# q, k and v of the second block as three 1024-column groups with three steps of seven products each

## The chip, the cores and the metric

The kernel runs on one core of a Trainium2 chip. The metric is the device time of one execution in microseconds, as a median of several runs. The engines are TensorE (PE in the profile, its weight loads PEld), VectorE (DVE), ScalarE (ACT), GpSimd (POOL) and SyncE (SP), which issues the loads.

## What is computed

Two transformer blocks follow one another on 256 tokens of 2048 features in float32. The parts that matter here, shortened:

```python
def rms_norm(x, g):
    y = x * lax.rsqrt(jnp.mean(x * x, axis=-1, keepdims=True) + EPS)
    return y * g

def first_block(x, ...):                         # DEPTH = 1, mixer 0
    h = rmsnorm(x, norm_g[i, 0])
    h = fox_attention(h, fox_w_in[j], fox_b_f[j], fox_w_out[j])
    x = x + rmsnorm(h, norm_g[i, 1])
    h = sqrelu_mlp(rmsnorm(x, norm_g[i, 2]), mlp_w1[i], mlp_w2[i])
    return x + rmsnorm(h, norm_g[i, 3])

def hybrid_layer(x, norm_g, w_in, ...):          # the second block
    h = rms_norm(x, norm_g)
    proj = h @ w_in
    q, k, v, z_a, u_b, v_b, z_b, g_a, g_b = jnp.split(proj, cuts, axis=-1)
    q = rms_norm(q.reshape(B, S, 8, 128), q_norm_g)
    k = rms_norm(k.reshape(B, S, 8, 128), k_norm_g)
    att = moba_attention(q, k, v.reshape(B, S, 8, 128))
    y_a = (att * silu(z_a)) @ w_proj_a
    sgu = spatial_gating(gelu(u_b), gelu(v_b), sgu_norm_g, w_s, b_s)
    y_b = (sgu * silu(z_b)) @ w_proj_b
    merged = sigmoid(g_a) * y_a + sigmoid(g_b) * y_b
    return x + merged @ w_out
```

The change concerns `h @ w_in` for the first 3072 columns of `w_in` (q, k and v), the head norms' sums of squares of q and k, and the end of the v_b columns, which come just before them.

## The kernel before

**Products in parts.** Every float32 matrix product is made in three matmuls on values split in a rounded part and a rest: x_hi w_hi + x_lo w_hi + x_hi w_lo. The activations lie turned (features on partitions) in `h_both` or `a_both`. The weights come as a stream of 622 chunks of 128x1024 floats (512 KB) through a ring of four slots `raw`. For each chunk SyncE issues the load as soon as VectorE has made `w_lo` of the chunk four before in the same slot; ScalarE makes `w_hi` (`split`, L935), but not before TensorE has finished the chunk four before (`chunk_done`); VectorE makes `w_lo = raw - w_hi` (`rest`, L1412). The call `next_split(c)` or `next_rest(c)` handles chunk c + 4. Each engine runs its program in the written order, and semaphores tie them together.

**Groups.** In the phase `qkv` (64 chunks) TensorE first does v_b in `first_groups` (chunks 0 to 15, 1024 columns in two halves, `group_bank[0]` and `group_bank[1]`), where the first chunks run beside the turning of the normed input. Chunks 8 to 11 finish the first half and 12 to 15 the second. Then `rows_of_rstd(3)` (L659) makes rows of the row scales `rstd` in bank 6. It waits for `diagonal(3)`, which VectorE makes when GpSimd has computed `rstd` (`pow_norm`) from the sums of squares that `scale_of_rows(2)` adds up. Then come q, k and v as six groups of 512 columns, each 8 chunks, two groups to a turn of a loop (`group_pair`, chunks 16 to 63). After each group ScalarE squares the two banks (L1307), and VectorE scales them into `qkv` (L1967) and adds the squares up by head (L1970). The stage behind is `sgu_uz` (feature tiles).

**v_b's gelu.** Each half is scaled and squared by ScalarE, multiplied out by VectorE, put through tanh by ScalarE and summed by head, with roundings of later chunks between.

**Wide groups.** The MLP's second product is already done in groups of 1024 columns, 16 chunks, each with three steps of seven products (`seven_products`). A step takes a 2x2 arrangement of blocks (two feature blocks by two halves of the tokens, two feature blocks by two halves of the columns) and makes seven block products in place of eight, by Winograd's form of Strassen's rule. It needs four sums of activations for each step (`x_forms`, rounded by ScalarE into `x_form_hi`, VectorE's rest in `x_form_lo`), three sums of weights for each step and group (`outer_sums`, `inner_sum`, `last_sum`; `form_hi` on ScalarE, `form_rest` on VectorE), and a join of the four extra sums at the group's end (`join_seven`, then `plain_drain`). The three sums and the difference written back over `raw` come before the split of the step's first chunk.

## Time and profile before

| | us |
|---|---|
| median of 3 runs | 1782.65 (1782.48 to 1783.97) |
| the profiled execution, whole | 1782.02 |
| its span, first to last instruction | 1780.3 |
| TensorE busy | 1772.9 |
| VectorE busy | 1234.5 |
| ScalarE busy | 869.1 |
| GpSimd busy | 139.6 |

Times in the profile are us from the span's start. A matmul's end is modelled and overlaps the next one's start, so that distances between starts tell the pace. In the timeline rows neighbouring operations of one kind are merged, with their count at the end. In the trace of this execution chunk 8 of the phase `qkv` begins at 1117 us and chunk 16, the first of q, at 1139 us.

### The profile page before, as it was taken

To read this page: it belongs to the slowest core of one execution; us is meant where nothing else is said; L and a number is where in the kernel's file an instruction comes from. 1 tells how busy PE (TensorE), PEld (TensorE's weight loads), DVE (VectorE), ACT (ScalarE), POOL (GpSimd) and SP (SyncE) were. 2 spreads that over 40 slices of the span, in tenths; PEclk is the share of its full clock that TensorE was granted. 3 is DMA by queue.
4 is the path that set the end of the run, shared out by engine and by line. 5 is a ranking of instruction groups with operands and counts; after the bars stand their busy time and mean duration, and the time that the engine had idled before them with its cause. 6 is when DMAs were issued, how large, how long until landed. Compare 5 with 4: busy or idle time off the path is not lost.

```text
span 1780.3 us, 26370 instructions
## 1 busy us (share of the span) xinstructions
PE 1772.9 (100%) x8818; PEld 1503.3 (84%) x8818; DVE 1234.5 (69%) x1623; ACT 869.1 (49%) x1169; POOL 139.6 (8%) x190
## 2 busy tenths in 40 slices
PE   9999999999999999999999999999999999999999
PEld 8888888888888888888888887888888888888887
DVE  6567777556888788778887868755688655555654
ACT  7434444446555445445554555744444445553442
POOL 1012121000001000000000000100013011000000
PEclk9999999999999999999999999999999999999999
DMA  8665455556568656855775586555555655555554
GB/s 326 206 219 163 165 165 165 190 169 193 171 212 228 200 186 214 232 191 189 214 235 189 189 251 199 191 196 190 179 186 177 201 174 180 172 175 189 186 189 154
DMA packets 99111, 347.24 MB, mean 195 GB/s; under 512 B 11472, under 2 KB 11872, under 8 KB 98656
## 3 DMA queue, kind: packets, MB, share of 16 engines
q1 hardware_dynamic: 93392, 333.23, 56.8%
q0 software_dynamic: 4784, 12.60, 3.3%
q8 instruction: 47, 0.77, 0.2%
q10 hardware_dynamic: 864, 0.44, 0.1%
q14 instruction: 24, 0.20, 0.0%
HBM read 336.77 MB, written 2.11 MB: 190 GB/s over the span
## 4 chain that ended last, share of the span: by engine, by line
PE 95%; DVE 2%; DMA 1%; issue 1%; ACT 1%; POOL 0%; SPq 0%; DVEq 0%; ACTq 0%; POOLq 0%
PE bank L457 39%; PE bank L436 23%; PE bank L441 12%; PE bank L750 5%; PE bank L751 5%; PE bank L749 5%; DMA raw<-in_stream 1%; PE bank L473 1%; PE bank L507 1%; PE bank L586 1%; DVE w_lo L1412 1%; PE bank L627 1%; PE bank L642 1%; ACT w_hi L935 1%; PE bank L633 0%
## 5 line engine op out<-in xcount | busy, mean ns | idle before, releaser
L1412 DVE TENSOR_TENSOR w_lo<-raw,w_hi 128x1024 fp32r<-128x1024 f32 x620 | 755.3, 1225 | 423.5 <-ACT w_hi L935 420.1
L935 ACT ACTIVATE w_hi<-raw 128x1024 fp32r<-128x1024 f32 x620 | 649.3, 1056 | 622.5 <-PE bank L457 336.6
L457 PE MATMUL bank<-w_hi,h_both 128*128 128x512 f32 x1544 | 480.0, 392 | 0.0
L436 PE MATMUL bank<-h_both,w_hi 128*128 128x512 f32 x1792 | 432.8, 394 | 0.4 <-DVE gate L1815 0.4
L436 PEld LDWEIGHTS bank<-h_both,w_hi 128*128 128x128 f32 x1792 | 330.6, 188 | 65.9 <-issue 0.9
L457 PEld LDWEIGHTS bank<-w_hi,h_both 128*128 128x128 f32 x1544 | 288.0, 188 | 58.3
L457 PE MATMUL bank<-w_lo,h_both 128*128 128x512 f32 x772 | 301.1, 390 | 0.0
L441 PEld LDWEIGHTS bank<-h_both,w_lo 128*128 128x128 f32 x1792 | 229.8, 191 | 8.7
L441 PE MATMUL bank<-h_both,w_lo 128*128 128x256 f32 x1792 | 232.5, 283 | 0.0
L457 PE MATMUL bank<-w_hi,a_both 128*128 128x512 f32 x576 | 178.5, 391 | 0.0
L457 PEld LDWEIGHTS bank<-w_lo,h_both 128*128 128x128 f32 x772 | 145.0, 188 | 30.4
L457 PEld LDWEIGHTS bank<-w_hi,a_both 128*128 128x128 f32 x576 | 107.5, 188 | 21.8
L749 PE MATMUL bank<-w_hi,a_both 128*128 128x512 f32 x322 | 125.6, 390 | 0.2 <-DVE w_lo L1412 0.2
L750 PE MATMUL bank<-w_hi,a_both 128*128 128x512 f32 x322 | 125.4, 390 | 0.0
L751 PE MATMUL bank<-w_lo,a_both 128*128 128x512 f32 x322 | 125.4, 389 | 0.0
L457 PE MATMUL bank<-w_lo,a_both 128*128 128x512 f32 x288 | 112.3, 390 | 0.0
L1173 ACT ACTIVATE a_both<-gate 128x256 fp32r<-128x256 f32 (+1 forms) x56 | 23.4, 418 | 139.6 <-DVE gate L1714 139.6
L749 PEld LDWEIGHTS bank<-w_hi,a_both 128*128 128x128 f32 x322 | 60.5, 188 | 13.5 <-issue 1.2
L751 PEld LDWEIGHTS bank<-w_lo,a_both 128*128 128x128 f32 x322 | 60.5, 188 | 12.5
L750 PEld LDWEIGHTS bank<-w_hi,a_both 128*128 128x128 f32 x322 | 60.5, 188 | 12.3
L457 PEld LDWEIGHTS bank<-w_lo,a_both 128*128 128x128 f32 x288 | 54.1, 188 | 11.3
L2238 POOL DMA_DIRECT2D wide<-scaled x21 | 18.4, 1000 | 540.6 <-ACT scaled L1212 540.6
(237 smaller groups left out, 1384.5 us busy)
## 6 DMA issues: line engine op xcount, KB each, us to landing
raw<-in_stream SPq DMA_DIRECT2D x622, 512.0 KB, 3.5
wide<-scaled POOLq DMA_DIRECT2D x21, 256.0 KB, 4.9
res<-in_x SPq DMA_DIRECT2D x4, 512.0 KB, 7.9
rowg<-in_norm_rows POOLq DMA_DIRECT2D x2, 1024.0 KB, 8.1
gate<-cum_rows POOLq DMA_DIRECT2D x1, 2048.0 KB, 8.3
out<-wide SPq DMA_DIRECT2D x8, 256.0 KB, 5.1
wide<-gate POOLq DMA_DIRECT2D x7, 256.0 KB, 8.6
gate<-in_x_turned SPq DMA_DIRECT2D x5, 256.0 KB, 6.4
```

The costliest lines, as they stand in the source:

```text
L436: pe.matmul(tile_sum[b][:, :], w_hi[:, slot + half, k * P:(k + 1) * P], h_both[:, 8 * half + k, :], start=half == 0 and k == 0, stop=False)
L441: mm = pe.matmul(tile_sum[b][:, 0:TOK], w_lo[:, slot + half, k * P:(k + 1) * P], h_both[:, 8 * half + k, 0:TOK], start=False, stop=half == ...
L457: mm = pe.matmul(dst[t][:, :], xt[:, k0 + 2 * j + k, tt], wt[:, slot, w], start=j == 0 and k == 0 and n == 0, stop=last and k == 1 and n == 2)
L473: mm = pe.matmul(dst[t][:, :], xt[:, 2 * j + k, tt], wt[:, slot, w], start=j == 0 and k == 0 and n == 0, stop=j == GROUP_CHUNKS - 1 and k ...
L507: mm = pe.matmul(group_bank[0][t][:, :], xt[:, 2 * j + k, t * P:(t + 1) * P], wt[:, j % RING, w], start=first, stop=False)
L749: pe.matmul(dst[:, :], x_parts[0], w_parts[0], start=start, stop=False)
L750: pe.matmul(dst[:, :], x_parts[1], w_parts[0], start=False, stop=False)
L751: return pe.matmul(dst[:, :], x_parts[0], w_parts[1], start=False, stop=stop)
L935: nc.scalar.activation(w_hi[:, slot, :], raw[:, slot, :], ACT.Copy).then_inc(hi_ready, 1)
L1173: nc.scalar.activation(one(a_hi, i * 2 + b), relu2[b], ACT.Copy).then_inc(ff_hi, 1)
L1412: nc.vector.tensor_tensor(w_lo[:, slot, :], raw[:, slot, :], w_hi[:, slot, :].bitcast(F32), ALU.subtract).then_inc(lo_ready, 1)
L2238: pool.dma_start(group_sum[:, t, start:start + GROUP_COLS], src, accum_op=ALU.add).then_inc(added[t][n], 16)
```

## The change

q, k and v become three wide groups of 1024 columns and 16 chunks, each with three steps of seven products, on banks `h_bank`. The shared functions take the activations, the form tiles and the banks as arguments now. The tiles for the forms lie in the space of `a_both`, which is free in this phase. The input forms are made from `h_hi + h_lo` by `h_forms`, between the roundings of chunks 12 to 15, and rounded by ScalarE between its splits. `rows_of_rstd(3)` moves two chunks forward, in front of chunk 14, and the copy of its rows (`keep_rows(2)`) into the first half of gelu, since bank 6 is one of the first group's banks. Roundings for the first wide group are woven into the second half of gelu. The results are joined in `h_part`, and ScalarE squares them head by head with accumulation (q and k only) and scales them into `qkv` (`scale_qkv`). VectorE's scaling and reductions of q, k and v go. The kernel's stream holds the same weights in another order. The core of the diff:

```diff
+        h_part = [gate_flat[:, 2048 + n * 512:2560 + n * 512] for n in range(4)]
+        h_sum = [gate_flat[:, 2048 + b * 256:2304 + b * 256] for b in range(2)]
+        qkv_forms = Forms(in_a("h_w_raw", 0, [3, GROUP_COLS], F32)[:, :, :], in_a("h_w_hi", 1536, [3, GROUP_COLS]),
+                          in_a("h_w_lo", 3072, [3, GROUP_COLS]), in_a("h_x_raw", 7680, [4, P], F32)[:, :, :],
+                          in_a("h_x_hi", 4608, [STEPS, 4, P]), in_a("h_x_lo", 6144, [STEPS, 4, P]), h_part)
...
+        h_bank = [[bank[2], bank[3], bank[7], bank[6]], [bank[0], bank[1], bank[5], bank[4]]]
...
+            def qkv_group(i):
+
+                c = FIRST["qkv"] + 16 + 16 * i
+                w = WIDE_GROUPS + i
+                plain, seven = h_bank[i % 2], h_bank[1 - i % 2]
+                if i:
+                    joined(w - 1)
+                else:
+                    pe.wait_ge(group_taken[0], 8)
+                for j in range(0, WIDE_CHUNKS, 2):
+                    pair = PAIR_ORDER[j // 2]
+                    if j in SEVEN_AT:
+                        if i:
+                            pe.wait_ge(join_step, 8 * w)
+                        else:
+                            pe.wait_ge(group_taken[1], 8)
+                        seven_products(c, j, SEVEN_AT.index(j), w, plain, seven, (h_hi, h_lo), qkv_forms,
+                                       STEPS * FF_GROUPS)
                         continue
                     for k in range(2):
-                        wide_chunk(c, j + k, 2 * pair + k, plain, g * 8 + 20 if n == 0 else 0)
+                        wide_chunk(c, j + k, 2 * pair + k, plain, (h_hi, h_lo),
+                                   {} if i else {3: lambda: pe.wait_ge(rows_ready, 2)})
...
-            first_groups(FIRST["qkv"], 6, 2)
-            rows_of_rstd(3)
-            with pe.Fori(1, 4) as i:
-                group_pair(FIRST["qkv"] + i * 16, i + 6, h_hi, h_lo)
+            first_groups(FIRST["qkv"], 6, 2, {(1, 6): lambda: rows_of_rstd(3)})
+            for i in range(QKV_WIDE):
+                qkv_group(i)
+            joined(WIDE_GROUPS + QKV_WIDE - 1)
 
...
             for m in range(4):
                 next_split(c + 8 + m)
+                if m < STEPS:
+                    act.wait_ge(x_form_step, 4 * STEPS * FF_GROUPS + 6 * m + 6)
+                    nc.scalar.activation(qkv_forms.x_hi[:, m, :, :], qkv_forms.x_raw, ACT.Copy).then_inc(x_form_hi_ready, 1)
...
+                vb_split(n, 2)
+                vb_split(n, 3)
+
+            def scale_qkv(i, t):
+
+                for n in range(2):
+                    block = 2 * t + n
+                    act.wait_ge(join_step, 8 * (WIDE_GROUPS + i) + block + 5)
+                    if i < 2:
+                        if 4 * i + block >= 2:
+                            act.wait_ge(qkv_sq, 4 * i + block - 1)
+                        for head in range(4):
+                            ins = nc.scalar.activation(gelu_a[:, n, head * P:(head + 1) * P],
+                                                       h_part[block][:, head * P:(head + 1) * P], ACT.Square,
+                                                       scale=rstd[:, t:t + 1],
+                                                       accum_out=head_sq[:, t, i * 8 + 4 * n + head:i * 8 + 4 * n + head + 1])
+                        ins.then_inc(qkv_sq, 1)
+                    start = i * 1024 + n * GROUP_COLS
+                    nc.scalar.activation(qkv[:, t, start:start + GROUP_COLS], h_part[block], ACT.Copy,
+                                         scale=rstd[:, t:t + 1]).then_inc(qkv_in, 1)
+
+            act.wait_ge(vb_sums, 4)
+            for i in range(QKV_WIDE):
+                for j in range(0 if i else RING, WIDE_CHUNKS):
+                    wide_split(c + 16 + 16 * i, WIDE_GROUPS + i, j, qkv_forms, h_bank[1 - i % 2])
+                    if i and j < 2:
+                        scale_qkv(i - 1, j)
+            for t in range(NT):
+                scale_qkv(QKV_WIDE - 1, t)
...
+            def wide_step(c, w, q, forms, drain=None):
+
+                at = SEVEN_AT[q]
+                step = STEPS * w + q
+                outer_sums(step, c + at, at % RING, forms)
+                if drain:
+                    drain(0, 0)
+                inner_sum(step, at % RING, forms)
+                if drain:
+                    drain(0, 1)
+                last_sum(step, at % RING, forms)
+                if drain:
+                    drain(1, 0)
+                    drain(1, 1)
+                for k in range(2):
+                    rest(c + at - RING + k, (at + k) % RING)
+                form_rest(step, forms)
+                for k in range(2, 4):
+                    rest(c + at - RING + k, (at + k) % RING)
+
+            def wide_join(c, w, seven, part):
+
+                rests(c + 12, range(2))
+                join_seven(w, seven, part)
+                rests(c + 12, range(2, RING))
...
+            def h_forms(q):
+
+                done = 4 * STEPS * FF_GROUPS + 6 * q
+                for b in range(2):
+                    kt = 2 * SEVEN_PAIRS[q] + b
+                    nc.vector.tensor_tensor(h_sum[b], h_hi[:, kt, :].bitcast(F32), h_lo[:, kt, :].bitcast(F32),
+                                            ALU.add).then_inc(x_form_step, 1)
+                a11, a21 = [h_sum[0][:, t * P:(t + 1) * P] for t in range(NT)]
+                a12, a22 = [h_sum[1][:, t * P:(t + 1) * P] for t in range(NT)]
+                s1, s2, s3, s4 = [qkv_forms.x_raw[:, f, :] for f in range(4)]
+                dve.wait_ge(x_form_step, done + 2)
+                nc.vector.tensor_tensor(s1, a21, a22, ALU.add).then_inc(x_form_step, 1)
+                nc.vector.tensor_tensor(s3, a11, a21, ALU.subtract).then_inc(x_form_step, 1)
+                dve.wait_ge(x_form_step, done + 3)
+                nc.vector.tensor_tensor(s2, s1, a11, ALU.subtract).then_inc(x_form_step, 1)
+                dve.wait_ge(x_form_step, done + 5)
+                nc.vector.tensor_tensor(s4, a12, s2, ALU.subtract).then_inc(x_form_step, 1)
+
+            def h_forms_lo(q):
+
+                dve.wait_ge(x_form_hi_ready, STEPS * FF_GROUPS + q + 1)
+                nc.vector.tensor_tensor(qkv_forms.x_lo[:, q, :, :], qkv_forms.x_raw,
+                                        qkv_forms.x_hi[:, q, :, :].bitcast(F32),
+                                        ALU.subtract).then_inc(x_form_ready, 1)
+
+            dve.wait_ge(chunk_done, c)
             next_rest(c + 8)
+            h_forms(0)
             next_rest(c + 9)
             scale_of_rows(2)
+            h_forms_lo(0)
+            h_forms(1)
             next_rest(c + 10)
+            h_forms_lo(1)
+            h_forms(2)
             next_rest(c + 11)
+            h_forms_lo(2)
             diagonal(3)
...
                     next_rest(c + 13)
+                    keep_rows(2)
+                else:
+                    next_rest(c + 17)
...
+                    outer_sums(STEPS * WIDE_GROUPS, c + 20, 0, qkv_forms)
+                    inner_sum(STEPS * WIDE_GROUPS, 0, qkv_forms)
+                    last_sum(STEPS * WIDE_GROUPS, 0, qkv_forms)
+                else:
+                    form_rest(STEPS * WIDE_GROUPS, qkv_forms)
+                    next_rest(c + 18)
+                    next_rest(c + 19)
+
+            for i in range(QKV_WIDE):
+                for q in range(0 if i else 1, STEPS):
+                    wide_step(c + 16 + 16 * i, WIDE_GROUPS + i, q, qkv_forms,
+                              (lambda t, n: qkv_drain(i - 1, t, n)) if i and q == 0 else None)
+                wide_join(c + 16 + 16 * i, WIDE_GROUPS + i, h_bank[1 - i % 2], h_part)
+            for t in range(NT):
+                for n in range(2):
+                    qkv_drain(QKV_WIDE - 1, t, n)
+
+
+            dve.wait_ge(qkv_in, 4 * QKV_WIDE)
...
-    parts += [paired_groups(v_b)] + [token_groups(m) for m in (q, k, v)]
+    parts += [paired_groups(v_b)] + [wide_groups(m) for m in (q, k, v)]
```

Line numbers in the changed kernel differ from those of before.

Where TensorE stands at the end of v_b, chunks 14 and 15 and the row scales (`qk_norm,ones`), before, from the last matmuls of chunk 15 to the first of q:

```order
L457 MATMUL bank<-w_lo,h_both 128x512
L457 MATMUL bank<-w_hi,h_both 128x512 x2
L457 MATMUL bank<-w_lo,h_both 128x512
L457 MATMUL bank<-w_hi,h_both 128x512 x2
L457 MATMUL bank<-w_lo,h_both 128x512
L659 MATMUL bank<-qk_norm,ones 128x128 [waits diag_ready]
L659 MATMUL bank<-qk_norm,ones 128x128
L841 UNCONDITIONAL_BRANCH
L841 ISA
L447 ISA [waits group_taken0]
L457 MATMUL bank<-w_hi,h_both 128x512 [waits lo_ready]
```

and in the changed kernel, from the end of chunk 13 to chunk 14:

```order
L472 MATMUL bank<-w_lo,h_both 128x512
L472 MATMUL bank<-w_hi,h_both 128x512 x2
L472 MATMUL bank<-w_lo,h_both 128x512
L472 MATMUL bank<-w_hi,h_both 128x512 x2
L472 MATMUL bank<-w_lo,h_both 128x512
L676 MATMUL bank<-qk_norm,ones 128x128 [waits diag_ready,h_ready]
L676 MATMUL bank<-qk_norm,ones 128x128
L472 MATMUL bank<-w_hi,h_both 128x512 [waits lo_ready]
L472 MATMUL bank<-w_hi,h_both 128x512
L472 MATMUL bank<-w_lo,h_both 128x512
L472 MATMUL bank<-w_hi,h_both 128x512 x2
```

The wait for `diag_ready` stood behind chunk 15 and stands behind chunk 13 now.

VectorE in the same place, before, from the roundings of chunks 11 to 13 to the diagonal (`qk_norm<-ident,rstd`):

```order
L1412 TENSOR_TENSOR w_lo<-raw,w_hi 128x1024 [waits hi_ready] x3
L1474 TENSOR_REDUCE sq_all<-sq_sum 128x2 [waits sumsq_ready]
L1412 TENSOR_TENSOR w_lo<-raw,w_hi 128x1024 [waits hi_ready] x2
L1479 TENSOR_SCALAR qk_norm<-ident,rstd 128x128 [waits rstd_ready]
L1479 TENSOR_SCALAR qk_norm<-ident,rstd 128x128
L1925 TENSOR_SCALAR mean_sq<-rstd 128x2
```

and now, the last lap: chunk 14's rounding, the low part of the second set, the third set (`h_x_raw`), chunk 15's rounding and the diagonal:

```order
L1486 TENSOR_TENSOR w_lo<-raw,w_hi 128x1024 [waits hi_ready]
L2029 TENSOR_TENSOR h_x_lo<-h_x_raw,h_x_hi 128x512 [waits x_form_hi_ready]
L2013 TENSOR_TENSOR gate<-h_both 128x256 x2
L2019 TENSOR_TENSOR h_x_raw<-gate 128x128 [waits x_form_step]
L2020 TENSOR_TENSOR h_x_raw<-gate 128x128
L2022 TENSOR_TENSOR h_x_raw<-h_x_raw,gate 128x128 [waits x_form_step]
L2024 TENSOR_TENSOR h_x_raw<-gate,h_x_raw 128x128 [waits x_form_step]
L1486 TENSOR_TENSOR w_lo<-raw,w_hi 128x1024 [waits hi_ready]
L2029 TENSOR_TENSOR h_x_lo<-h_x_raw,h_x_hi 128x512 [waits x_form_hi_ready]
L1553 TENSOR_SCALAR qk_norm<-ident,rstd 128x128 [waits rstd_ready]
L1553 TENSOR_SCALAR qk_norm<-ident,rstd 128x128
L2046 TENSOR_SCALAR mean_sq<-rstd 128x2
```

Between each rounding and the next there are now seven operations on the input forms, with a wait for ScalarE's rounding (`x_form_hi_ready`).

ScalarE at a group's end before: the fourth split of a ring and the two squares of a 512-column group, with the loop's register work:

```order
L935 ACTIVATE w_hi<-raw 128x1024 [waits raw_landed2,chunk_done]
L933 REGISTER_ALU
L935 ACTIVATE w_hi<-raw 128x1024 [waits raw_landed3,chunk_done]
L1306 REGISTER_ALU
L1307 ACTIVATE gate<-bank,rstd 128x512 [waits qkv_sums]
L1306 REGISTER_ALU
L1307 ACTIVATE gate<-bank,rstd 128x512 [waits qkv_sums]
```

and now at the start of k, from the split of its chunk 4 (which waits for `form_step`) on:

```order
L978 ACTIVATE w_hi<-raw 128x1024 [waits raw_landed0,chunk_done,form_step]
L1366 ACTIVATE gate,head_sq<-gate,rstd 128x128 [waits join_step]
L1366 ACTIVATE gate,head_sq<-gate,rstd 128x128 x3
L1372 ACTIVATE wide<-gate,rstd 128x512
L1366 ACTIVATE gate,head_sq<-gate,rstd 128x128 [waits join_step]
L1366 ACTIVATE gate,head_sq<-gate,rstd 128x128 x3
L1372 ACTIVATE wide<-gate,rstd 128x512
L978 ACTIVATE w_hi<-raw 128x1024 [waits raw_landed1,chunk_done]
L1233 ACTIVATE h_w_hi<-h_w_raw 128x1536 [waits forms_done,form_step]
L1366 ACTIVATE gate,head_sq<-gate,rstd 128x128 [waits qkv_sq,join_step]
L1366 ACTIVATE gate,head_sq<-gate,rstd 128x128 x3
L1372 ACTIVATE wide<-gate,rstd 128x512
```

The squares by head (`gate,head_sq`, four to a block) and the scaled copies (`wide<-gate,rstd`) stand between the splits of chunks 4 and 5, and again behind the rounding of the weight forms, in front of the split of chunk 6.

## Rows read from the trace of the kernel before

**Rows 1.** The page: busy time of the engines, and the clock slices (40).
```profile
PE 1772.9 (100%) x8818; PEld 1503.3 (84%) x8818; DVE 1234.5 (69%) x1623; ACT 869.1 (49%) x1169; POOL 139.6 (8%) x190
...
PEclk9999999999999999999999999999999999999999
```
**Rows 2.** Waits of TensorE: who waited for whom, us in total, times, longest.
```profile
PE bank L500 <- POOL ident L2152: 1.7, 1, 1.7
```
**Rows 3.** Timeline of TensorE: start us, duration us, engine, line, operation, out<-in, count.
```profile
1128.06 0.62 PE L457 MATMUL bank<-w_hi,h_both 128*128 128x512 f32 x2
...
1133.50 0.62 PE L457 MATMUL bank<-w_hi,h_both 128*128 128x512 f32 x2
...
1138.95 0.61 PE L659 MATMUL bank<-qk_norm,ones 128*128 128x128 f32 x4
1139.31 0.48 PE L457 MATMUL bank<-w_hi,h_both 128*128 128x512 f32 x1
```
**Rows 4.** Timeline of VectorE under v_b; in brackets its idle time before.
```profile
1121.54 1.23 DVE L1412 TENSOR_TENSOR w_lo<-raw,w_hi 128x1024 fp32r<-128x1024 f32 x1 [1.15 <-ACT w_hi L935]
...
1125.05 0.15 DVE L1474 TENSOR_REDUCE sq_all<-sq_sum 128x2 f32<-128x8 f32 x1
1126.63 1.80 DVE L1412 TENSOR_TENSOR w_lo<-raw,w_hi 128x1024 fp32r<-128x1024 f32 x1 [1.43 <-ACT w_hi L935]
...
1130.49 0.48 DVE L1479 TENSOR_SCALAR qk_norm<-ident,rstd 128x128 f32<-128x128 f32 x2
```
**Rows 5.** Timeline of VectorE, input forms of the MLP.
```profile
478.27 0.42 DVE L1717 TENSOR_TENSOR a_both<-gate,a_both 128x256 fp32r<-128x256 f32 x1 [0.48 <-ACT a_both L1173]
478.62 0.28 DVE L1736 TENSOR_TENSOR wide<-gate 128x128 f32<-128x128 f32 x1
...
479.55 1.22 DVE L1412 TENSOR_TENSOR w_lo<-raw,w_hi 128x1024 fp32r<-128x1024 f32 x1
480.68 0.69 DVE L1725 TENSOR_TENSOR x_form_lo<-wide,x_form_hi 128x512 fp32r<-128x512 f32 x1
```
**Rows 6.** Timeline of ScalarE, the same place.
```profile
479.67 0.63 ACT L1182 ACTIVATE x_form_hi<-wide 128x512 fp32r<-128x512 f32 x1 [0.48 <-DVE wide L1741]
```
**Rows 7.** Timeline of ScalarE, start of a wide group of the MLP.
```profile
533.88 1.05 ACT L935 ACTIVATE w_hi<-raw 128x1024 fp32r<-128x1024 f32 x1
534.83 1.47 ACT L1198 ACTIVATE form_hi<-gate 128x1536 fp32r<-128x1536 f32 x1
536.21 0.71 ACT L1212 ACTIVATE scaled<-scaled,rstd_sq 128x512 f32<-128x512 f32 x1
536.82 0.71 ACT L1212 ACTIVATE gate<-gate,rstd_sq 128x512 f32<-128x512 f32 x1
```
**Rows 8.** Timeline of GpSimd under v_b.
```profile
1126.26 1.09 POOL L2260 TENSOR_SCALAR_AFFINE_SELECT gate<-gate 128x1024 f32<-128x1024 f32 x1
```
**Rows 9.** Timeline of VectorE: first and last of gelu's second half, and the copy after.
```profile
1141.39 0.43 DVE L1931 TENSOR_SCALAR gate<-gate 128x512 f32<-128x512 f32 x1
...
1146.40 0.41 DVE L1484 COPY rstd_rows<-bank 128x256 f32<-128x256 f32 x1
```
**Rows 10.** Timeline of VectorE, start of a wide group of the MLP.
```profile
530.13 0.68 DVE L1762 TENSOR_TENSOR gate<-raw 128x512 f32<-128x512 f32 x1
...
534.93 2.35 DVE L1412 TENSOR_TENSOR w_lo<-raw,w_hi 128x1024 fp32r<-128x1024 f32 x2
537.21 1.75 DVE L1780 TENSOR_TENSOR form_lo<-gate,form_hi 128x1536 fp32r<-128x1536 f32 x1
```
**Rows 11.** Timeline of ScalarE, exponentials with accumulation.
```profile
1423.24 0.38 ACT L957 ACTIVATE prob<-logit,neg_max 128x128 f32<-128x128 f32 x1
1423.53 0.19 ACT L957 ACTIVATION_READ_ACCUMULATOR prob<-logit,neg_max 128x1 f32 x1
1423.62 0.49 ACT L959 ACTIVATE prob<-logit,neg_max 128x256 f32<-128x256 f32 x1
```
**Rows 12.** The page, DMA issues: KB each, median us to landing.
```profile
raw<-in_stream SPq DMA_DIRECT2D x622, 512.0 KB, 3.5
```

More of the change, by code:

```diff
@@ L13 @@
+import collections
 from contextlib import ExitStack
@@ L42 @@
 WIDE_GROUPS = 7
+QKV_WIDE = 3
 EPS = 1e-6
@@ L770, in wide_chunk @@
                     for n in range(2):
[L771 to L773 removed]
+                        if first and 2 * t + n in bank_free:
+                            bank_free[2 * t + n]()
+                        x_block = [part[:, kt, t * P:(t + 1) * P] for part in x]
+                        mm = product(plain[2 * t + n], x_block, w_block(j % RING, n), first, last)
                     if last and t == 0:
```

239 lines of the change are left out of this document (105 added, 134 removed).

## The prediction, made before the changed kernel was run

> **What bounds the kernel now.** I read the page first. TensorE shows as busy for all of the span [rows 1]. Its matmuls overlap, so that alone proves little. The second view is TensorE's waits: its longest wait in the whole program is 1.7 us, in the opening, before any product [rows 2]. The third is its timeline around the stage that changes. Chunk 12 of this stage starts at 1128.06 and chunk 14 at 1133.50: 24 matmuls of 128x512 in 5.44 us, 0.2267 us each, end to end [rows 3]. (I number chunks from the stage's start: 0 to 15 are v_b; q, k and v are 16 to 63; 12 matmuls each, 2.72 us.) So the kernel's time is the number of matmuls times their spacing. A matmul removed is a gain only as long as VectorE and ScalarE go on delivering split weights before TensorE asks, and any wait put in front of TensorE is paid in full. I therefore price the arithmetic first and then lay out three places where the two helpers get more to do before a fixed due time.
>
> **Products removed.** Three groups have three steps each, and each step makes 7 block products in place of 8. A product is 3 matmuls, so 9 x 3 = 27 matmuls go: 27 x 0.2267 = **6.1 us** saved. The 549 left in q, k and v keep their shape and their spacing. The matmuls of the row scales, four short ones that take 0.36 us from 1138.95 to the next product [rows 3], are only moved. Loads of weights stay 512 KB each.
>
> **Place 1, under v_b: the input forms.** VectorE now makes three sets of input forms between the roundings of chunks 12, 13, 14 and 15, and only then the diagonal for which TensorE waits with the row scales. TensorE's wait also stands two chunks earlier, in front of chunk 14, due at 1133.50. Before, VectorE ended the diagonal at 1130.49 + 0.48 = 1130.97 [rows 4], 2.5 us ahead even of the new place. Now the two helpers hand work back and forth. VectorE's forms of set n must be done before ScalarE rounds them, and ScalarE rounds them before it splits chunk 13 + n, and VectorE needs that split for its next rounding. One lap:
> - two additions of 256 columns, 0.35 each by the distance of the first two rows of [rows 5], about 0.1 for the hand-over, and four of 128 in 479.55 - 478.62 = 0.93: 1.75 to 1.85 us;
> - ScalarE's rounding of the 512 columns, 0.63 [rows 6], with its split (1.05) starting some 0.55 into it, since its operations follow 0.95 apart where each takes 1.05 [rows 7]: 1.6;
> - VectorE's rest of the split, 1.14 to the next start (480.68 - 479.55 is 1.13), and the low part of the forms, 0.6 to 0.7 [rows 5];
> - hand-overs between engines, 0.03 twice.
> That is 5.3 us. The first lap begins when VectorE has done chunk 12, about 1122.7 (1121.54 + 1.14) [rows 4]. The laps end at 1128.0, 1133.3 and 1138.5, and the diagonal's two operations at 1138.9. TensorE is late by 1138.9 - 1133.5 = 5.4 us. Something comes on top: GpSimd's mask of w_s, 1.09 us, starts 1.2 us behind VectorE's sum of the row statistics [rows 4, 8]. That sum now comes at 1127.4 in place of 1125.05, so the mask falls on the second lap's additions. Before, the same mask fell on a rounding of VectorE that took 1.80 in place of 1.23 [rows 4]: 0.6 us, which I add, with 0 and 1.1 as its ends. With 0.1 for TensorE to start again: **+6.1 us** (4.5 to 6.7). The low end is for shorter small additions in a lap.
>
> The Trainium skill's "SBUF — State Buffer", section "Who interferes with whom", says a VectorE operation with two inputs in SBUF is held by a GpSimd operation that reads SBUF for all of that operation. By that rule the addition is the mask's whole 1.1 us, where the row gives 0.6, and the sum would be 0.5 us higher.
>
> **Place 2, the first step of q.** After the diagonal VectorE must do both halves of v_b's gelu, the roundings of chunks 16 to 21, four sums of weight blocks and the low part of the weight forms before TensorE can begin the last three products of chunks 20 and 21. A half of gelu takes 1146.40 - 1141.39 = 5.0 us, of which some 0.4 is waiting that other work can now fill [rows 9]; six roundings at 1.14, four sums at 0.6 to 0.7 and the form's low part of 1.75 [rows 10] make 11.2; the copy of the row scales 0.3. Together 20.7 to 21.6 us after the diagonal. TensorE needs 0.1 + 0.36 + chunks 14 to 19 (16.3) + four products (2.7) = 19.5 us to be there. So it waits 1.2 to 2.1; I take **+1.5 us** (0 to 2.5). Both chains start at the diagonal, so place 1 doesn't hide it.
>
> **Place 3, the start of k and of v.** ScalarE now squares the previous group by heads. Call T TensorE's start of the group. The rounding of chunk 3 waits for the end of the group before: it is done at T + 2.4 (split 1.06, rest 1.23). VectorE's eight sums and drains stand 0.6 apart (530.13 to 534.93) [rows 10], so two of them are done at T + 3.7 and release the split of chunk 4 (ScalarE). Behind that split stand two blocks, each of four squares with accumulation and one scaled copy. An activation of 128 columns with accumulation and its read take 1423.62 - 1423.24 = 0.38 [rows 11], the copy of 512 takes 0.61 (536.21 to 536.82) [rows 7]: 4 x 0.38 + 0.61 = 2.13 a block. ScalarE: T + 3.7, split to 4.7, two blocks to 9.0, split of chunk 5 to 9.9, form of 1536 columns (1.38) to 11.3 [rows 7], two blocks to 15.6, and only then the split of chunk 6, done at 16.7; VectorE's rest makes it T + 17.9. TensorE is due there after four chunks and seven products, 10.88 + 4.76 = T + 15.6. Late by 2.3, at k and again at v: **+4.6 us**. In the wide groups of the MLP this place holds four scaled copies (2.4 us) and no squares, which is why it doesn't show there. With 0.35 a square each wait is 1.8; with a read that isn't overlapped (0.38 + 0.19) it is 5. At the group's next step the helpers are back in time: a step is 10.2 us of TensorE against 4 sums, 4 roundings and a form, 9.1 us of VectorE.
>
> **What I cost at nothing.** The joins run under the group's last two chunks, 5.4 us for four additions and two roundings. Weight loads land 3.5 us after issue [rows 12], inside the 9.1 us cycle. Behind v there are no squares, and TensorE has two tiles in hand, 11 us, while ScalarE makes four copies (2.4). If that cover fails it would cost 1 to 2 us. VectorE's 12 scalings and 12 reductions of q, k and v go; they were not in TensorE's way.
>
> **The sum.** -6.1 + 6.1 + 1.5 + 4.6 = +6.1 us. The profiled execution took 1782.02 us, 1.7 more than its span of 1780.3; it would become 1788.1. The median of the runs is 0.6 higher, 1782.65, so the forecast is 1788.7.
>
> **Rivals.**
> - Arithmetic alone, faster. The laps of place 1 don't reach TensorE and the squares fit. Then only the 6.1 us remain: 1776.5. For it: no wait of TensorE in the MLP's groups of the same build is over 1.7 us [rows 2]. Against it: three laps would have to fit between 1122.7 and 1133.5, 3.6 us each where the rows give 5.3. It decides at a total of waits under 2.5 us. Chance 0.07.
> - Even. Place 1 is as worked out or a little less, but places 2 and 3 cost half (squares shorter from SBUF than the exponentials of [rows 11], gelu's waits filled): -6.1 + 5.4 + 3 = +2.3, 1785.0. Between 1779.1 and 1786.2. Chance 0.26.
> - The clock. At place 1 TensorE would stand idle for some 6 us in one piece, and the trace has no such gap after its opening; the granted clock is at its full level, 2.4 GHz, in every slice [rows 1], so no row shows what such a gap does. If it fell to 1.2 GHz, one or two chunks (14, 15) would run at twice the spacing, +2.7 to +5.4, of which place 2 gives back up to 1.5 because VectorE gains that time. Net +1.2 to +3.9: about 1791. Chance 0.17. The Trainium skill's "TensorE: Matmul & The Clock Gate", section "Part 1: The HAM clock gate", speaks for it: an idle TensorE goes back to the lower of its two clocks and has to be busy again before it is released. No run here shows it yet.
>
> **How the numbers follow.** Forecast 0.50, clock 0.17, even 0.26, arithmetic alone 0.07. About 0.2% (3.6 us) is what a measurement of this kernel can tell from no change. Slower by more is the first two, 0.67; within it 0.26; faster 0.07. The range leaves out the arithmetic alone and the far ends of the squares: from the even case with the low ends (-6.1 + 4.5 + 0 + 1.8 = +0.2, 1782.5) to the clock case, 1792.5.
>
> **What would show it.** In the changed kernel's waits of TensorE: one of 5 to 7 us at the row scales' matmul on the diagonal; one of 1 to 2 at the first low part of the weight forms; two of about 2.3 on the rounding of chunk 6 of k and of v. VectorE's timeline should show three idle times of about 1.8 us in front of the roundings of chunks 13 to 15, with ScalarE named. A granted clock below 1.0 after 1139 would show the third rival. Wrong would be: a diagonal done before 1134, squares under 0.3 us each, or a total of waits in the stage below 9 us.

## The result, and the profile after

The changed kernel takes **1793.64 us** (median of 5 runs, 1789.77 to 1795.19) against 1782.65 (5 runs, 1780.79 to 1783.97): ratio 1.0056, 95% interval 1.0042 to 1.0071. It is slower, by more than was forecast (1788.7, with a range up to 1792.5). The profiled execution took 1793.69, its span is 1792.0.

First the page, against [rows 1]:

```profile
PE 1772.9 (99%) x8791; PEld 1500.4 (84%) x8791; DVE 1279.3 (71%) x1689; ACT 895.0 (50%) x1248; POOL 140.7 (8%) x190
...
PEclk9999999999999999999999999999999999999999
```

TensorE has 27 matmuls fewer, as it should, and yet the same busy time. The clock line shows nothing, since a slice of 45 us is too coarse. Next TensorE's waits under and behind v_b (engine, line, what it waited for: us in total, times, longest):

```profile
PE bank L676 <- DVE qk_norm L1553: 6.8, 1, 6.8
PE bank L766 <- DVE w_lo L1486: 4.4, 2, 2.2
```

The first is place 1 of the prediction, the second place 3 at k and at v. Here is TensorE at place 1 (start, duration; in brackets the idle time):

```profile
1133.58 0.39 PE L472 MATMUL bank<-w_lo,h_both 128*128 128x512 f32 x1
1140.75 1.20 PE L676 MATMUL bank<-qk_norm,ones 128*128 128x128 f32 x4 [6.78 <-DVE qk_norm L1553]
1141.60 1.20 PE L472 MATMUL bank<-w_hi,h_both 128*128 128x512 f32 x2
1142.59 0.63 PE L472 MATMUL bank<-w_lo,h_both 128*128 128x512 f32 x1
1143.02 1.05 PE L472 MATMUL bank<-w_hi,h_both 128*128 128x512 f32 x2
...
1145.02 0.40 PE L472 MATMUL bank<-w_lo,h_both 128*128 128x512 f32 x1
```

The wait is one thing to see. The other stands behind it: from 1142.59 to 1143.02 are 0.43 us, where [rows 3] has 0.2267 from matmul to matmul. The eight intervals from 1141.60 to 1145.02 take 3.42 us in place of 1.81. At k the same happens:

```profile
1205.93 0.39 PE L768 MATMUL bank<-h_w_lo,h_both 128*128 128x512 f32 x1
1208.54 0.50 PE L766 MATMUL bank<-w_hi,h_both 128*128 128x512 f32 x1 [2.22 <-DVE w_lo L1486]
...
1210.30 0.63 PE L766 MATMUL bank<-w_hi,h_both 128*128 128x512 f32 x1
1210.73 0.63 PE L767 MATMUL bank<-w_hi,h_both 128*128 128x512 f32 x1
```

The table of stretches says why (window, its length, busy us and count of PE, PEld, DVE, ACT, POOL, then TensorE's granted clock, DMA share, GB/s):

```profile
1100.00:1133.00 33.00, 33.00 (x156) 27.25 (x155) 24.91 (x42) 20.95 (x40) 2.40 (x3) 1.00 0.57 188
...
1138.00:1145.00 7.00, 4.25 (x12) 3.58 (x13) 6.55 (x12) 6.24 (x10) 0.00 (x0) 0.51 0.22 75
1145.00:1200.00 55.00, 54.91 (x242) 45.16 (x241) 50.12 (x59) 33.99 (x52) 9.38 (x6) 1.00 0.61 192
...
1209.70:1213.10 3.40, 3.40 (x10) 2.63 (x9) 3.33 (x5) 2.25 (x3) 0.00 (x0) 0.50 0.84 261
...
1254.00:1257.50 3.50, 3.34 (x8) 2.66 (x9) 3.43 (x6) 1.02 (x2) 0.00 (x0) 0.51 0.49 154
```

Behind each of the three waits TensorE runs at the lower of its two levels, 1.2 GHz, for some eight products.

With this the 11.7 us between the spans (1792.0 - 1780.3) can be laid out from starts of matmuls. A gap counts as what it has above 0.2267, and the first product behind a wait, which the next follows 0.1 later than usual, is counted with the wait:

| | forecast | profile after |
|---|---|---|
| 27 products less | -6.1 | -6.1 |
| place 1, wait for the diagonal | +6.1 | +6.9 |
| place 2, first weight forms of q | +1.5 | +0.35 |
| place 3, wait at chunk 6 of k, of v | +2.3, +2.3 | +2.5, +2.5 |
| low clock behind place 1 (row scales 0.5, products 1.6) | 0 | +2.1 |
| low clock behind the waits of k and v | 0 | +1.6, +1.6 |
| sum | +6.1 | +11.4 |

So the waits come to 12.25 us, where I had said 12.2. That they agree so well is partly luck: place 1 is 0.8 above its term and place 3 0.4, and place 2 is 1.15 below. What is left is the clock, 5.3 us.

VectorE under v_b shows the laps (idle time in brackets), and GpSimd its mask:

```profile
1122.39 1.23 DVE L1486 TENSOR_TENSOR w_lo<-raw,w_hi 128x1024 fp32r<-128x1024 f32 x1 [1.22 <-ACT w_hi L978]
1123.53 0.76 DVE L2013 TENSOR_TENSOR gate<-h_both 128x256 f32<-128x256 f32 x2
...
1126.99 1.23 DVE L1486 TENSOR_TENSOR w_lo<-raw,w_hi 128x1024 fp32r<-128x1024 f32 x1 [1.65 <-ACT w_hi L978]
...
1129.80 1.21 DVE L2020 TENSOR_TENSOR h_x_raw<-gate 128x128 f32<-128x128 f32 x1
...
1133.19 1.23 DVE L1486 TENSOR_TENSOR w_lo<-raw,w_hi 128x1024 fp32r<-128x1024 f32 x1 [1.65 <-ACT w_hi L978]
...
1138.38 1.23 DVE L1486 TENSOR_TENSOR w_lo<-raw,w_hi 128x1024 fp32r<-128x1024 f32 x1 [1.64 <-ACT w_hi L978]
...
1140.13 0.47 DVE L1553 TENSOR_SCALAR qk_norm<-ident,rstd 128x128 f32<-128x128 f32 x2
```
```profile
1129.78 1.09 POOL L2383 TENSOR_SCALAR_AFFINE_SELECT gate<-gate 128x1024 f32<-128x1024 f32 x1
```

From rounding to rounding is a lap: 6.2 us for the one with the mask in it, 5.2 for the next. And ScalarE at the start of k, the first square with its read, the next square, the first copy, the next block's first square, the last copy and the split for which TensorE waits:

```profile
1195.23 0.39 ACT L1366 ACTIVATE gate<-gate,rstd 128x128 f32<-128x128 f32 x1
1195.53 0.19 ACT L1366 ACTIVATION_READ_ACCUMULATOR gate<-gate,rstd 128x1 f32 x1
1195.62 0.39 ACT L1366 ACTIVATE gate<-gate,rstd 128x128 f32<-128x128 f32 x1
...
1196.78 0.71 ACT L1372 ACTIVATE wide<-gate,rstd 128x512 f32<-128x512 f32 x1
1197.39 0.39 ACT L1366 ACTIVATE gate<-gate,rstd 128x128 f32<-128x128 f32 x1
...
1205.57 0.71 ACT L1372 ACTIVATE wide<-gate,rstd 128x512 f32<-128x512 f32 x1
1206.18 1.99 ACT L978 ACTIVATE w_hi<-raw 128x1024 fp32r<-128x1024 f32 x2
```

A block of four squares and a copy takes 1197.39 - 1195.23 = 2.16 us, and ScalarE has no idle time from the split of chunk 4 (1194.27) to that of chunk 6. The split of chunk 6 starts at 1206.18, when TensorE is already there (1205.93 + 0.23).

### The profile page after: what moved, and what is told of

The parts are those of the page before. It is cut to its first block, busy times and chain, and to the rows that moved or that the text cites. A ratio compares the mean times of both kernels' runs of the same rounds, so it can differ in the third digit from the quotient of the medians.

```text
span 1792.0 us, 26289 instructions
## 1 busy us (share of the span) xinstructions
PE 1772.9 (99%) x8791; PEld 1500.4 (84%) x8791; DVE 1279.3 (71%) x1689; ACT 895.0 (50%) x1248; POOL 140.7 (8%) x190
## 4 chain that ended last, share of the span: by engine, by line
PE 90%; DVE 4%; ACT 3%; issue 2%; DMA 2%; POOL 0%; SPq 0%; ACTq 0%; DVEq 0%; POOLq 0%
PE bank L472 30%; PE bank L451 23%; PE bank L456 12%; PE bank L766 6%; PE bank L768 6%; PE bank L767 6%; DMA raw<-in_stream 2%; ACT w_hi L978 2%; DVE w_lo L1486 1%; PE bank L522 1%; PE bank L488 1%; ACT gate L1366 1%; PE bank L644 1%; PE bank L659 1%; PE bank L601 0%
## 5 line engine op out<-in xcount | busy, mean ns | idle before, releaser
L472 PE MATMUL bank<-w_hi,h_both 128*128 128x512 f32 x1160 | 362.8, 394 | 0.0
L472 PEld LDWEIGHTS bank<-w_hi,h_both 128*128 128x128 f32 x1160 | 216.5, 189 | 43.7
L472 PE MATMUL bank<-w_lo,h_both 128*128 128x512 f32 x580 | 226.6, 391 | 0.0
L472 PEld LDWEIGHTS bank<-w_lo,h_both 128*128 128x128 f32 x580 | 109.2, 188 | 23.3
(278 smaller groups left out, 1793.6 us busy)
```

What stands on the lines that cost most here:

```text
L472: mm = pe.matmul(dst[t][:, :], xt[:, k0 + 2 * j + k, tt], wt[:, slot, w], start=j == 0 and k == 0 and n == 0, stop=last and k == 1 and n == 2)
```

## The experiments

All times are medians, each beside runs of the kernel before on the same chip. These gave 1781.66 for the first four experiments, 1781.58 for the next four and 1781.43 for the last four. The part of the program ahead of the change scatters too: the last product before the row scales starts at 1133.58 in the profile of the changed kernel and at 1131.60 in that of the next kernel. That wait also differs between executions: it is 6.8 us in the profile above, and 6.3 in the other five of this document that do the same work up to there and leave the wait unfilled. So single spans are compared only where that start is taken off.

**Squares and copies moved behind the splits** of chunks 6, 7, 10 and 11, one block behind each.

```diff
-                    if i and j < 2:
-                        scale_qkv(i - 1, j)
+                    if i and j in (2, 3, 6, 7):
+                        scale_qkv(i - 1, [(2, 3, 6, 7).index(j)])
```

> The changed kernel with one edit: at k and v, ScalarE does the four blocks of squares and scaled copies behind the splits of its chunks 6, 7, 10 and 11 of the group (one block each), in place of two blocks in front of the split of chunk 5 and two in front of that of chunk 6. Theory A (the squares in front of the split make TensorE wait 2.4 us at each of k and v, and each of those gaps lowers the clock for the next 8 matmuls): both waits and both spells at 1.2 GHz go, 8.5 us less than the changed kernel, about 1785.1 us. Theory B (those waits come from weight loads or from the drains, whatever ScalarE does): within 1 us of the changed kernel, 1793.

Measured: 1784.22 (1783.08 to 1786.19), ratio 1.0016 (1.0006 to 1.0025). No wait is left at k or v, and TensorE's only one is

```profile
PE bank L676 <- DVE qk_norm L1552: 6.3, 1, 6.3
```

The kernel before is 2.6 us away, where the changed kernel was 10.4 to 11.0 away. So place 3 costs about 8 us, not the 4.6 that was forecast for its waits; from starts of matmuls it is 4.1 + 4.0 in the profile of the changed kernel.

**Input forms one place later.** The diagonal comes ahead of the third set of forms. ScalarE rounds the first set behind its next split, and the other two in the first half of gelu. The part of VectorE up to the diagonal:

```diff
             next_rest(c + 9)
             scale_of_rows(2)
             h_forms_lo(0)
-            h_forms(1)
             next_rest(c + 10)
-            h_forms_lo(1)
-            h_forms(2)
+            h_forms(1)
             next_rest(c + 11)
-            h_forms_lo(2)
             diagonal(3)
```

> The changed kernel with one edit: VectorE makes only the first two sets of input forms before the diagonal, neither in the way of a split, and ScalarE rounds them behind splits; the third set and the low part of the second move into the first half of gelu. Squares as in the changed kernel. Theory A (the hand-over laps hold up the diagonal): the diagonal is ready near 1132, the wait of 6.8 us and its 1.7 us of low clock go, the wait at the first weight forms grows from 0.3 to some 1.5 to 2.7 us: about 1786 to 1787 us. Theory B (the diagonal is late for another reason, such as GpSimd): the wait stays over 5 us, 1792.

Measured: 1785.02 (1783.20 to 1786.58), ratio 1.0019 (1.0010 to 1.0029), 1 us below what was expected. Place 1 is gone, the waits are

```profile
PE bank L766 <- DVE w_lo L1495: 5.1, 3, 2.2
PE bank L766 <- DVE h_w_lo L1864: 1.3, 1, 1.3
```

This profile holds two equal waits with different outcomes. At k and at v the last product before and the first behind the wait stand 2.6 us apart. At k the clock stays high, at v it falls:

```profile
1198.00:1208.00 10.00, 7.78 (x35) 6.08 (x33) 8.19 (x9) 7.32 (x10) 0.00 (x0) 1.00 0.42 129
...
1244.90:1248.20 3.30, 3.14 (x7) 2.51 (x8) 3.23 (x6) 0.82 (x1) 0.00 (x0) 0.50 0.58 169
```

The ten runs sort themselves by their mean granted clock: 1783.7 on average for the three at 1.000, 1785.1 for the five at 0.999, 1786.1 for the two at 0.998. If each step of 0.001 is one fall, as in this profile (0.999, one fall), that is 1.0 to 1.4 us for each.

**Both repairs.**

> The two edits together. Theory A: 27 matmuls fewer and one wait of 1 to 3 us left at the first weight forms: 1777.5 to 1779.5 us, or 1.7 more if that wait lowers the clock. If the effects hang together (what one place gives up another takes), over 1782.

Measured: 1777.87 (1777.33 to 1779.99), ratio 0.9981 (0.9971 to 0.9990), faster than the kernel before. The clock is 1.00 throughout. What is left are two short waits in q's first step:

```profile
PE bank L766 <- DVE h_w_lo L1863: 1.4, 1, 1.4
PE bank L766 <- DVE w_lo L1494: 0.6, 1, 0.6
```

From starts of matmuls place 2 is 2.8 us here, and -6.1 + 2.8 = -3.3 against the measured -3.8.

**TensorE kept busy at place 1.** 56 turns (transposes) of the unit matrix in front of the wait for the diagonal, into a bank that nobody reads before it is begun anew. All waits stay.

```diff
+                if norm == 3:
+                    for _ in range(56):
+                        pe.transpose(tile_sum[0][:, 0:P], ident[:, :], ident[:, :])
```

> The changed kernel, but TensorE does 56 transposes of the identity into a free bank in front of its wait for the diagonal, about 6 us of work that nobody uses, in the gap of 6.8 us. Theory A (the clock falls because TensorE stands idle): the first product behind the row scales starts at the same time as in the changed kernel, its matmuls are 0.227 us apart in place of 0.427, 1.6 us less: about 1792. The gaps at k and v keep their low clock. Theory B (short transposes don't count as work, or the clock falls for another reason): the spacing stays 0.427 us there, 1793.6.

Measured: 1790.06 (1789.09 to 1790.50), ratio 1.0047 (1.0030 to 1.0063). The clock stays high at place 1 and still falls at k:

```profile
1131.00:1145.00 14.00, 13.89 (x93) 12.36 (x92) 12.22 (x24) 9.74 (x14) 0.00 (x0) 1.00 0.35 112
...
1206.50:1209.90 3.40, 3.40 (x9) 2.64 (x9) 3.33 (x5) 2.29 (x3) 0.00 (x0) 0.50 0.83 276
```

Place 2 now costs 1.5 us (1.59 and 0.34 from start to start, less 2 x 0.2267), where it was 0.35. The low clock had hidden it, since VectorE gained that time.

The expectation was 1792, with the low clock left at k and v in every run. In the profile, where both are there, the stretch from the last product before the row scales to the end is 1788.8 - 1131.65 = 657.1 us, in the changed kernel 1792.0 - 1133.58 = 658.4: 1.3 less. The median is nearer to the kernel before by 2.0 to 2.6. The mean clocks of the four runs (0.998, 0.999, 0.999, 1.000) say why: only the first has room for two falls.

**Ten products of zeros in front of chunk 6 of k and v.** `ones` is set to zero once the row scales have been made.

```diff
+                    if i and j == SEVEN_AT[0] + 2:
+                        pe.wait_ge(zeros_made, 1)
+                        for _ in range(10):
+                            pe.matmul(plain[0][:, :], ones[:, :], h_both[:, 0, :],
+                                      start=False, stop=False)
```

> The changed kernel, in which TensorE does ten more products of 128x512 ahead of the wait for chunk 6 of k and as many at v. They take a stationary block of zeros and are added to the first plain bank, so that nothing is changed in what is computed; 10 x 0.227 = 2.3 us fill the wait of 2.4. Nothing else moves. Theory A, the low clock behind each wait is a cost of its own: no stretch at 1.2 GHz at k and v, the eight products behind chunk 6 are 0.227 us apart and not 0.427, and each place gives back 8 x 0.2 = 1.6 us or a little more; the next weights are not late. Against the changed kernel (1793.6) 3.2 to 4 us less, some 1790, 8 to 9 us above the kernel before. Rival B, the low clock only uses up time that a later wait would have taken anyway: the clock stays high, and a new wait of 1 to 2 us stands at the weight forms behind chunk 6; the time stays within 1 us of 1793.6. Rival C, the clock falls for another reason than the idle time: the stretches at 1.2 GHz stay.

Measured: 1790.08 (1788.99 to 1790.51), ratio 1.0049 (1.0034 to 1.0065). TensorE goes from the zeros to chunk 6, no later than before, and on at full pace:

```profile
1204.62 2.49 PE L864 MATMUL bank<-h_both,ones 128*128 128x512 f32 x10
1207.00 0.50 PE L767 MATMUL bank<-w_hi,h_both 128*128 128x512 f32 x1
```

The stretch around it has a granted clock of 1.00, and so has the one at v:

```profile
1205.00:1216.00 11.00, 11.00 (x50) 8.82 (x49) 10.21 (x11) 6.92 (x7) 0.00 (x0) 1.00 0.53 165
```

The same stretch is 1787.3 - 1131.90 = 655.4 us here, against 658.4: 3.0 less, where the two falls were 3.2 (at place 1 this profile has a shorter wait, by 0.5, and three more slow products, 0.6, which nearly cancel). No new wait has taken that over, so rivals B and C fall.

**Both fillings.**

> The kernel with ten products of zeros ahead of chunk 6 of k and v, and with the 56 turns of the unit matrix ahead of the row scales too. Nothing but TensorE's idle time is filled; every wait keeps its length. Theory A: granted clock 1.00 in the whole run, so that what is left above the kernel before is the waits alone: the two kinds of filling add up. 1790.1 (turns alone) less 3.2 to 4 is 1786.3 to 1787.2, 4.5 to 5.5 us above the kernel before; that is also what the prediction's sum was without the clock (1788.7, of which 1 us is the scatter of the kernel before). Rival B, the cost of the clock is taken over by waits: 1789 or more.

Measured: 1788.57 (1788.14 to 1790.42), ratio 1.0043 (1.0028 to 1.0058), and a granted clock of 1.000 in every run. This is 1.4 us above the 1787.2 that theory A allowed, and under rival B's 1789. I had taken off both falls of the clock at k and v from a kernel, turns alone, whose four runs (0.998 to 1.000) had had about one of the two. TensorE has work at place 1 until the row scales:

```profile
1133.33 6.28 PE L677 MATMUL bank<-ident 128*128 128x128 f32 x56
1139.71 0.71 PE L680 MATMUL bank<-qk_norm,ones 128*128 128x128 f32 x4
```

It is the prediction's own case, all waits and no low clock: 7.0 us above the kernel before, where the sum was 6.1. From starts of matmuls it is -6.1 + 6.4 + 1.2 + 2.5 + 2.5 = 6.5, which is also the difference of the two spans (1786.8 - 1780.3).

**Only the squares moved**, the copies left where the change has them (`square_heads` is the four squares of a block):

```diff
                     if i and j < 2:
                         scale_qkv(i - 1, j)
+                    if i and j in (2, 3, 6, 7):
+                        square_heads(i - 1, (2, 3, 6, 7).index(j))
```

> The changed kernel, in which only the squares with the sums by head (four of 128 columns for each block of q and k) are moved behind the splits of chunks 6, 7, 10 and 11; the four scaled copies of 512 columns stay where the change put them, ahead of the split of chunk 6. Theory A, it is the squares that make chunk 6 late, as the prediction said: no wait of over 0.5 us at chunk 6 of k and v, no low clock there, the time that of the kernel with squares and copies moved, 1784.2 +- 1. Rival B, copies and squares are alike to blame: a wait of about half (1.0 to 1.5 us) stays at chunk 6 of k and v, with or without the low clock: 1786.5 to 1790.

Measured: 1784.46 (1783.42 to 1785.58), ratio 1.0016 (1.0006 to 1.0025), the same as with the copies moved. No wait stands at k or v, the only one from v_b to the end of v is

```profile
PE bank L676 <- DVE qk_norm L1558: 6.3, 1, 6.3
```

So the copies alone don't make chunk 6 late, and the wait of 1.0 to 1.5 us that rival B names isn't there. Whether the squares alone would is not shown: the four copies ahead of that split take 4 x 0.61 = 2.4 us, as much as TensorE waited, so that by the rows above (an estimate) moving the copies alone would about close the wait too. No run tried that.

**The second half of gelu in pieces** through q's steps, on top of both repairs. VectorE's part (ScalarE's tanh and squares stand behind the splits of chunks 7 and 13 of q):

```diff
+                    if SPREAD and i == 0:
+                        if q == 1:
+                            cube(1, 0)
+                            gelu_half(1, 0)
+                        else:
+                            sums_half(1, 0)
+                            cube(1, 1)
```

> The kernel with both repairs (input forms a place later, the row scales' diagonal ahead of them, squares and copies behind the splits), 1777.9, in which the second half of v_b's gelu is moved too: behind the roundings of the first weight forms of q, and in pieces through q's three steps, instead of ahead of them. Theory A, the 1.0 us and 1.7 us between products at the first weight forms and at q's first roundings come from that work on VectorE and ScalarE: both gaps go to 0.4 or less, 2.0 us less, 1775.5 to 1776.5. Rival B, the pieces make roundings of q late at another place by the same sum: gaps of 0.5 to 1.5 us further on in q, 1777 to 1779. If a gap of over 2 us comes, the clock falls too and it is 1780.

Measured: 1777.06 (1776.03 to 1778.12), ratio 0.9975 (0.9965 to 0.9984). Rival B is nearer. The waits at the first step are gone and come back further on in q, the longest on a sum of weights:

```profile
PE bank L767 <- DVE gate L1919: 1.1, 1, 1.1
PE bank L767 <- DVE w_lo L1511: 0.5, 1, 0.5
```

**GpSimd's mask moved** behind the sums of v_b, in the changed kernel:

```diff
             pool.wait_ge(sgu_in, 32)
-            nc.gpsimd.affine_select(out=w_s, in_=w_s, compare_op=ALU.is_ge, fill=0.0, base=0,
-                                    pattern=[[0, 8], [1, P]], channel_multiplier=-1).then_inc(w_s_ready, 1)
             pool.wait_ge(vb_sums, 4)
+            nc.gpsimd.affine_select(out=w_s, in_=w_s, compare_op=ALU.is_ge, fill=0.0, base=0,
+                                    pattern=[[0, 8], [1, P]], channel_multiplier=-1).then_inc(w_s_ready, 1)
```

> The changed kernel, in which GpSimd's mask of the spatial weights (1.09 us) comes behind the sums of v_b, so that it no longer stands beside VectorE's low part of the input forms (1.21 us for what takes 0.28 alone). Theory A, VectorE waits for the port as long as GpSimd's instruction runs: that low part takes 0.3, VectorE and the diagonal are 0.9 us earlier, the wait at the row scales is 6.0 instead of 6.9 between products' starts, and the time 0.9 us less. Rival B, ScalarE's high parts set the pace there, not VectorE: the wait stays within 0.3 us of 6.9 though the low part takes 0.3. The low clock behind the wait is there in both.

Measured: 1789.34 (1789.12 to 1791.26), ratio 1.0047 (1.0030 to 1.0064). The expectation names the wrong operation: what stood beside the mask was the second of the small additions (L2020), not the low part. It takes its usual time now, and the wait is shorter:

```profile
1128.38 0.28 DVE L2020 TENSOR_TENSOR h_x_raw<-gate 128x128 f32<-128x128 f32 x1
```
```profile
PE bank L676 <- DVE qk_norm L1553: 5.4, 1, 5.4
```

5.4 against 6.3 in the changed kernel on the same chip (below) is the 0.9 of theory A. The median is 2.5 lower, more than 0.9. In this profile only five products behind the row scales run slow and v has no low clock. Whether the shorter wait brought that, four runs don't tell.

**Five products of zeros in place of ten.**

> As the kernel with ten products of zeros ahead of chunk 6 of k and v, but with five: 5 x 0.227 = 1.1 us of the wait are filled, and some 1.2 us stay idle. Theory A, a wait of 1 to 1.7 us leaves the clock alone (no stretch at 1.2 GHz followed the 1.0 and 1.7 us at the first steps of q in the kernel with both repairs): no low clock at k and v, time as with ten, 1790 +- 0.7. Rival B, any such wait near other idle time can lower it: stretches at 1.2 GHz stay at k or v in some runs, 1791 to 1793.

Measured: 1789.44 (1788.19 to 1790.45), ratio 1.0042 (1.0026 to 1.0059), level with ten. A gap of 1.45 us from start to start is left at k and at v, and the clock stays in this profile:

```profile
PE bank L767 <- DVE w_lo L1492: 2.1, 2, 1.1
```
```profile
1206.00:1216.00 10.00, 8.95 (x39) 7.03 (x39) 8.79 (x9) 7.32 (x8) 0.00 (x0) 1.00 0.44 155
```

**The second half of gelu in one piece** behind q's first roundings, on top of both repairs.

> The kernel with both repairs, in which the second half of v_b's gelu stands behind the roundings of q's first weight forms in one piece, not spread over q's steps. Theory A, one piece of some 8 us on VectorE in a place where it is ahead of TensorE by less makes q's next roundings late once: one gap of 1 to 2 us, 1776.5 to 1778. Rival B, the piece is longer than what VectorE is ahead, and TensorE waits over 2 us, with the low clock behind it: 1779 to 1781.

Measured: 1777.02 (1775.92 to 1778.26), ratio 0.9974 (0.9965 to 0.9984), as theory A has it and level with the pieces. One wait is left:

```profile
PE bank L767 <- DVE w_lo L1511: 1.5, 1, 1.5
```

**The changed kernel again**, beside the last three.

> The changed kernel itself once more, beside the kernels with zeros filled in and with the mask moved, on the same chip. Both theories: 1790 to 1795 with a granted clock of 0.996 to 0.998, runs with fewer stretches at 1.2 GHz at the lower end. If filling the waits at k and v helps by the clock alone, this is 2.5 to 4 us above them in runs with all three stretches, and level with them in runs with only the first.

Measured: 1791.81 (1789.51 to 1792.72), ratio 1.0057 (1.0040 to 1.0074). Its profile shows a low clock at k but none at v, with the same wait of 2.2 at both:

```profile
PE bank L676 <- DVE qk_norm L1553: 6.3, 1, 6.3
PE bank L766 <- DVE w_lo L1486: 4.4, 2, 2.2
```
```profile
1208.30:1211.70 3.40, 3.40 (x10) 2.62 (x9) 3.33 (x6) 2.05 (x3) 0.00 (x0) 0.50 0.93 269
1250.00:1260.00 10.00, 7.78 (x35) 6.08 (x34) 8.23 (x9) 7.32 (x10) 0.00 (x0) 1.00 0.41 117
```

All nine runs of the changed kernel together: at a mean clock of 0.996 they took 1792.6 to 1795.2 (five runs), at 0.997 and 0.998 they took 1789.5 to 1791.0 (four). So the clock goes with most of its scatter. The two kernels with zeros (1790.08, 1789.44) lie 1.7 and 2.4 us below this median, and level with the runs at 0.997 and 0.998, as expected.

## Why the prediction failed

The direction and the places were right. The time was not: 1793.6 lies 4.9 above the forecast and 1.1 above the range. **The step that failed is the treatment of the clock.** The sum had it at nothing. It stood as a rival with a chance of 0.17, for place 1 alone, and the 2.3 us waits of place 3 were never asked the question. It fell behind all three waits, for 5.3 us in the profile. The range had its upper end at the clock case for one place, which is why it was too low. (Its lower end holds a slip that changed nothing: a wait of 1.8 at k and at v is 3.6, and only 1.8 was added.)

- **Products**: 27 gone, x8818 to x8791. With the waits mostly removed (1777.0) 4.4 of the 6.1 us are realised. The other 1.7 are at the one wait left in that kernel (1.84 and 0.31 us between starts of products, less 2 x 0.2267), so the term was right.
- **Place 1**: 5.4 us for the laps, 0.6 for the mask and 0.1 were forecast, 6.9 measured in the first profile and 6.5 in the five others that leave the wait unfilled. A lap without the mask took 5.2, as worked out (5.3). The mask cost 0.93 (1.21 in place of 0.28 for an addition), not 0.6; moving it took 0.9 off the wait. The Trainium skill's "SBUF — State Buffer", section "Who interferes with whom", has the addition held for all of the mask's time. The trace speaks for it (mask 1129.78 to 1130.87, addition 1129.80 to 1131.01), and against my term taken from a rounding that overlapped it in another way. With 0.93 in place of 0.6 the term is 6.4, against the 6.5 of those five. The 0.5 us more of the first profile is scatter of that execution: the first lap starts 10.05 us before the last product there and 10.52 in the profile of the changed kernel again.
- **Place 2**: 1.5 forecast, 0.35 measured, but 1.2 to 1.5 as soon as the clock is held up at place 1. The term was right for the case that I had summed. The rival's remark that place 2 gives back up to 1.5 of the clock's cost was right too (0.9 to 1.1).
- **Place 3**: 2.3 at each forecast, 2.5 measured. A square with its read takes 0.39 (0.38 forecast), a block 2.16 (2.13). Moving the squares alone removed both waits; the prediction named the squares, but the copies were part of the same sum.
- **Nothing for joins, loads and the end of v**: no wait of TensorE stands there.
- **The clock at place 1**: the rival said +2.7 to +5.4 for one or two chunks at half pace, net +1.2 to +3.9. The profile has eight products, not twelve to twenty-four, +2.1, net about +1.1 with what place 2 gives back. The granted clock went from 1.00 to 0.51 behind the wait. The Trainium skill's "TensorE: Matmul & The Clock Gate", section "Part 1: The HAM clock gate", says that an idle TensorE goes back to the lower clock, and the trace agrees. I gave too little weight to it.
- **Filled waits as the test**: with both fillings, and so no low clock in any run, the kernel is 7.0 us slower than before, the sum said 6.1. Of the 0.9 between them 0.4 stand in the profile (place 1 +0.3, place 2 -0.3, place 3 +0.4); the rest is within the scatter of the medians. Against the changed kernel on its two occasions (+11.0 and +10.4 over the kernel before) the clock is 3.4 to 4.0 us of the median, net of place 2. It is less than the profile's 5.3 since place 2 gives back some 0.9 and not every run has all three falls.

What stays open is why one wait of 2.2 us lowers the clock and an equal one in the same execution does not.

## What to carry to other kernels

Price a wait of TensorE at its length and then ask what clock the products behind it will get; this counts most where an operation is moved so that one long wait, or several of over 2 us, come to stand in a stream that had none. When helpers hand work back and forth (VectorE, ScalarE, VectorE), put what TensorE waits for ahead of the hand-overs, and put work that nobody waits for behind the next split, not ahead of it. With these two moves the same change went from 11 us slower to 3.8 us faster, and to 4.4 or 4.5 faster with gelu's second half moved too.

## What the runs showed of the hardware

- A wait of 2.2 us (2.6 from start to start) is enough to lower TensorE's clock, but not always: at k and not at v in one profile, at v and not at k in another. Of the ten such waits in five profiles seven were followed by the low clock. In the profiles none of the gaps of 1.0, 1.45, 1.7 and 1.8 us from start to start was followed by it.
- At 1.2 GHz a 128x512 product follows the other by 0.427 us, at 2.4 GHz by 0.227. Behind a wait of 2.2 us some eight products were slow, behind the one of 5.4 to 6.8 us between five and thirteen, in all seven profiles that have it.
- 56 turns of the 128x128 unit matrix over 6.3 us kept the granted clock at 1.00. The Trainium skill's "TensorE: Matmul & The Clock Gate", section "Part 4: PE-mode transpose", says that the full clock doesn't engage for transposes. Here they held a clock that was already at its full level; whether they would raise a low one no run shows.
- The low clock is partly paid back at the next place where TensorE would have waited: 0.35 us at place 2 in place of 1.2 to 1.5.
